# Second pass of the expert ups and the downs in one stage, with 256 instead of 192 tokens gathered row by row

## What is computed

```python
def one(xc):                                   # xc: normed tokens, 1024 wide
    ...                                        # 8 heads x top 16 of 128 x 128 experts: idx, g (softmax)
    act = gelu(einsum('nd,nhkd->nhk', xc, expert_u[idx]), approximate=False)
    return einsum('nhk,nhkd->nd', g * act, expert_v[idx])
```

## Time and profile before

| | us |
|---|---|
| median of 3 runs (2007.05 to 2012.56) | 2011.68 |
| the profiled execution: its own time | 2011.93 |
| its span in the profile | 2010.3 |
| mean granted TensorE clock | 0.977 |

### The profile page before, as it was taken

How to read it: one execution, slowest core, us unless ns; L and a number is a source line. 1 busy time by engine, 2 the same in 40 slices (tenths; PEclk the granted TensorE clock), 3 DMA queues, 4 the chain that set the end, 5 groups by cost and what they waited for, 6 DMA issues and landing times.

```text
span 2010.3 us, 39023 instructions
## 1 busy us (share of the span) xinstructions
PE 1904.8 (95%) x14702; PEld 1805.8 (90%) x14702; DVE 1390.1 (69%) x2528; ACT 856.2 (43%) x1119; POOL 1119.5 (56%) x755
## 2 busy tenths in 40 slices
PE   7988988888999999999999999999989999999998
PEld 6977764358999999999999999999989999999998
DVE  3669665432589888964446776465638999999996
ACT  4233664412213454556566555344433333333331
POOL 3323222223225888886768888778864555665630
PEclk8999999889999999999999999999998999999999
DMA  5434878761123777776867898998989999999993
GB/s 166 78 107 150 284 255 284 245 214 63 64 106 126 221 228 233 219 230 224 303 220 273 307 348 313 397 338 310 338 290 306 323 361 348 354 358 335 358 332 113
DMA packets 253534, 508.80 MB, mean 253 GB/s; under 512 B 51041, under 2 KB 172962, under 8 KB 232642
## 3 DMA queue, kind: packets, MB, share of 16 engines
q1 hardware_dynamic: 202930, 369.56, 54.3%
q0 software_dynamic: 44032, 134.35, 18.4%
q10 hardware_dynamic: 6416, 2.78, 1.0%
HBM read 442.77 MB, written 63.73 MB: 252 GB/s over the span
## 4 chain that ended last, share of the span: by engine, by line
PE 72%; DVE 10%; POOL 6%; DMA 4%; ACT 4%; issue 2%; DVEq 1%; SPq 1%; ACTq 0%; POOLq 0%
PE pair L1552 20%; PE pair L1553 20%; PE pair L1554 19%; PE pair L1883 4%; DVE conv L1082 3%; POOL w_lo L651 2%; PE pair L1697 2%; POOL v_rows L662 2%; DMA act<-acts 2%; DMA acts<-act_out 1%; POOL picked_a L655 1%; PE pair L1709 1%; DVE pair L1437 1%; DVE w_lo L1491 1%; PE pair L1749 1%
## 5 line engine op out<-in xcount | busy, mean ns | idle before, releaser
L1552 PE MATMUL pair<-x_hi,w_hi 128*128 128x256 f32 (+2 forms) x2560 | 752.5, 294 | 28.0 <-DVE x_lo L1038 16.2
L1553 PE MATMUL pair<-x_lo,w_hi 128*128 128x256 f32 (+2 forms) x2560 | 742.5, 290 | 0.0
L1554 PE MATMUL pair<-x_hi,w_lo 128*128 128x256 f32 (+2 forms) x2560 | 741.0, 289 | 0.0
L1552 PEld LDWEIGHTS pair<-x_hi,w_hi 128*128 128x128 f32 x2560 | 487.0, 190 | 33.5 <-issue 18.8
L1553 PEld LDWEIGHTS pair<-x_lo,w_hi 128*128 128x128 f32 x2560 | 486.4, 190 | 0.2
L1554 PEld LDWEIGHTS pair<-x_hi,w_lo 128*128 128x128 f32 x2560 | 484.7, 189 | 0.0
L1552 PE MATMUL pair<-a_hi,w_hi 128*128 128x352 f32 x1024 | 332.5, 325 | 12.9 <-DVE w_lo L1491 9.7
L662 POOL DMA_INDIRECT v_rows<-in_v_t,at_row x192 | 199.4, 1039 | 238.0 <-DVE pair L1437 205.2
L1553 PE MATMUL pair<-a_lo,w_hi 128*128 128x352 f32 x1024 | 331.5, 324 | 0.0
L1554 PE MATMUL pair<-a_hi,w_lo 128*128 128x352 f32 x1024 | 331.2, 323 | 0.0
L651 POOL TENSOR_TENSOR w_lo<-w_raw,w_hi 128x1024 fp32r<-128x1024 f32 x116 | 275.7, 2399 | 87.5 <-ACT w_hi L922 87.4
(11 more groups left out here) (219 smaller groups left out, 2735.6 us busy)
## 6 DMA issues: line engine op xcount, KB each, us to landing
w_raw<-in_u_t SPq DMA_DIRECT2D x85, 1024.0 KB, 5.6
v_raw<-in_u_t SPq DMA_DIRECT2D x43, 1024.0 KB, 5.3
w_raw<-in_v_t SPq DMA_DIRECT2D x128, 256.0 KB
v_raw<-in_v_t SPq DMA_DIRECT2D x128, 256.0 KB
gates<-g_out SPq DMA_DIRECT2D x11, 2048.0 KB, 10.7
act<-acts SPq DMA_DIRECT2D x64, 352.0 KB, 5.9
g_in<-gates SPq DMA_DIRECT2D x16, 1408.0 KB, 10.5
acts<-act_out SPq DMA_DIRECT2D x64, 288.0 KB, 7.1
```

Of the source, the lines that this page charges most:

```text
L1552: te.matmul(out, s_hi, m_hi, start=start, stop=False)
L1553: te.matmul(out, s_hi, m_lo, start=False, stop=False)
L1554: return te.matmul(out, s_lo, m_hi, start=False, stop=stop)
```

## The change

- NS becomes 256: tokens 0 to 255, which are those of pass one, are all gathered, in 2 x 128 slots; the dense part is 288 tokens, those of pass two. ALL_ROWS is 256. The move of half lists for 64 tokens (slots_moved) goes, and the list of token tile 1 is used as that of tile 0 is.
- Gates: 72 groups instead of 88, four in a step from step 46, so all within pass one.
- Pass two and the downs are one stage of 68 slots (ENDS). In a slot TensorE does half 0 of an up, block 0 of the down of the chunk four slots back (BESIDE), half 1, block 1. The gelus of the dense tokens stay in SBUF: no store and load of them.
- Split chunks of u and v take turns in three places (the third is x_hi/x_lo of the first 256 tokens, free by then); raw u and v have two buffers each. ups use PSUM banks 0 and 1, downs 2 and 3, one bank each.
- Low parts of u: on VectorE in the first four slots and then in two of three, else GpSimd. Low parts of v stay on VectorE. The 256 rows are spread evenly over the stage from its second step on.
- Outside: sigmoids at slot 15 instead of 20 and ahead of keep_output, finish_conv at 17 instead of 22, the copy of the next weights ahead of the square of a block instead of behind it.

```diff
-EXTRA = 64
-NS = P + EXTRA
+NS = FIRST
-GATES_FROM, GATES_PER_STEP = 47, 2
+GATES_FROM, GATES_PER_STEP = 46, 4
+BESIDE = 4
+ENDS = STEPS + BESIDE
+ROWS_FROM, ROWS_TO = 1, 63
 def on_vector(t):
-    return t % 4 == 0 if ROWS_FROM <= t < SPLIT_FROM else t >= SPLIT_FROM and t % 3 != 0
+    return t > STEPS and (t <= STEPS + BESIDE or t % 3 != 0)
+def rows_until(slot):
+    passed = (min(slot, BESIDE) + max(slot - STEPS, 0)) / 2 + max(min(slot, STEPS) - BESIDE, 0)
+    return int(min(max(ALL_ROWS * (passed - ROWS_FROM) / (ROWS_TO - ROWS_FROM), 0), ALL_ROWS))
+def gated_at(slot):
+    if slot < BESIDE:
+        return {2: (0, 1), 3: (2, 3)}.get(slot, ())
+    return (slot,) if slot < STEPS else ()
+def place_of_u(step):
+    return 2 * step % 3
+def place_of_v(c):
+    return (2 * (c + BESIDE) + 1) % 3
...
 # SP, after pass one
+            for parity in range(2):
+                sp.wait_ge(g_stored[parity], 16 * ((NG + 1 - parity) // 2))
+            load_gates(0, 0)
+            for parity in range(2):
+                sp.wait_ge(acts_stored[parity], 16 * STEPS // 2)
+            load_v(1)
+            load_gates(1, 1)
+            for slot in range(ENDS):
+                if slot + 3 < STEPS:
+                    wait_low_u(sp, STEPS + slot + 1)
+                    load_u(STEPS + slot + 3)
+                c = slot + 1 - BESIDE
+                if 0 <= c < STEPS - 2:
+                    sp.wait_ge(v_lo_done, c + 1)
+                    load_v(c + 2)
+                if slot % 4 == 3 and slot // 4 + 2 < STEPS // 4:
+                    sp.wait_ge(gated, 2 * slot + 2)
+                    load_gates(slot // 4 + 2, slot // 4 % 2)
 # GpSimd
+            for parity in range(2):
+                pool.wait_ge(acts_stored[parity], 16 * STEPS // 2)
+            for slot in range(ENDS):
+                for k in range(PIECE * slot, PIECE * slot + PIECE):
+                    if k < AHEAD:
                         fetch_unit(k)
+                mine = rows_added_at(slot)
+                for k in mine[:len(mine) // 2]:
                     fetch_ahead(k)
+                if slot + 1 < STEPS and not on_vector(STEPS + slot + 1):
+                    split_u(STEPS + slot + 1)
+                for k in mine[len(mine) // 2:]:
+                    fetch_ahead(k)
 # ScalarE
+            for slot in range(ENDS):
+                c = slot + 1 - BESIDE
+                if slot + 1 < STEPS:
+                    high_u(STEPS + slot + 1)
+                if slot < STEPS:
+                    gelu_out(STEPS + slot, 0)
+                    gelu_out(STEPS + slot, 1)
+                if 0 <= c < STEPS:
+                    high_v(c)
+                for step in gated_at(slot):
+                    high_a(step)
 # VectorE
+            for slot in range(ENDS):
+                c = slot - BESIDE
+                mine = rows_added_at(slot)
+                if c > 0:
+                    add_block(c - 1, 1)
+                if slot + 1 < STEPS and on_vector(STEPS + slot + 1):
+                    split_u(STEPS + slot + 1)
+                for k in mine[:len(mine) // 2]:
                     add_row(k)
+                if slot == TURN_FIRST + 2:
+                    add_total(0)
+                if c >= 0:
+                    add_block(c, 0)
+                for step in gated_at(slot):
+                    gate_acts(step)
+                if 0 <= c + 1 < STEPS:
                     split_v(c + 1)
+                for step in gated_at(slot):
+                    low_acts(step)
+                for k in mine[len(mine) // 2:]:
                     add_row(k)
 # TensorE
+            for slot in range(ENDS):
+                if slot == TURN_FIRST:
+                    turn_rows(0)
+                for half in range(2):
+                    if slot < STEPS:
+                        up(STEPS + slot, (half,))
+                    if slot >= BESIDE:
+                        down(slot - BESIDE, (half,))
```

More of the change, by code:

```diff
@@ L113, in splits_until, with u_buffer, u_loads, v_loads @@
     return mine if on_vector(t) else t + 1 - mine
-def stores_until(t):
-    return sum(32 if n < STEPS else 16 for n in range(t % 2, t + 1, 2))
+def u_buffer(t):
+    return t % 3 if t < STEPS else 1 - t % 2
+def u_loads(t):
+    return sum(1 for n in range(t + 1) if u_buffer(n) == u_buffer(t))
+def v_loads(c):
+    return c // 2 + 1
 def gate_groups(t):
@@ L355, in build_layer @@
     u_loaded = [sem(f"u_loaded{slot}") for slot in range(3)]
-    v_loaded = [sem(f"v_loaded{slot}") for slot in range(4)]
+    v_loaded = [sem(f"v_loaded{slot}") for slot in range(2)]
     g_loaded = [sem("g_loaded0"), sem("g_loaded1")]
@@ L373, in wait_low_u, with wait_place @@
         engine.wait_ge(u_lo_vector if on_vector(t) else u_lo_pool, 2 * splits_until(t) - 1 + j)
+    def wait_place(engine, step, c):
+        n = 2 * step if c is None else 2 * (c + BESIDE) + 1
+        engine.wait_ge(up_done, 2 * STEPS - 2 if n == 0 else 2 * STEPS)
+        for m in range(n - 3, -1, -3):
+            if m % 2 == 0 and m // 2 < STEPS:
+                engine.wait_ge(up_done, 2 * STEPS + m + 2)
+                return
+            if m % 2 and m // 2 >= BESIDE:
+                engine.wait_ge(down_done, 2 * (m // 2 - BESIDE) + 2)
+                return
     KEY_UNITS, VALUE_SLOTS = 12, 26
@@ L544, in _ @@
[L544 to L556, removed]
@@ L557, in _ @@
-            store_acts(PASSES - 1)
-            for parity in range(2):
[L559 to L570, removed]
-                    sp.wait_ge(v_lo_done, c + 1)
-                    load_v(2 * it + k // 4 + 1, k % 4)
-                if not last or k < 2:
-                    sp.wait_ge(a_done, 2 * c + 10)
-                    load_acts(c + 6, k % 2)
-                if not last and k % 4 == 3:
-                    sp.wait_ge(gated, 2 * c + 10)
-                    load_gates(2 * it + k // 4 + 3, (k // 4 + 1) % 2)
@@ L671, in fetch_ahead @@
                     fetch_row(k + RING)
-            for t in range(PASSES):
-                if not on_vector(t):
-                    split_u(t)
+            for t in range(STEPS + 1):
+                split_u(t)
                 if t == FETCH_FROM:
@@ L1895, in _ @@
             next_group = 3 * PH - 4
-            for t in range(PASSES):
+            for t in range(STEPS):
                 up(t)
@@ L1945, in _ @@
-            for quad in range(STEPS // 4 - 2, STEPS // 4):
-                for part in range(4):
-                    down(quad, quad % 2, part, quad == STEPS // 4 - 1 and part == 3)
+            te.wait_ge(rt_kept, NT - 2)
+            for slot in range(ENDS):
[6 more added lines that the diff above has]
+                        down(slot - BESIDE, (half,))
```

388 lines of the change are left out of this document (147 added, 241 removed).

## The result

The changed kernel takes 2014.93 us (median of 15 runs, 2008.65 to 2023.99); the kernel before took 2010.84 (15 runs). The ratio is 1.003 with a 95% interval of 1.0016 to 1.0044: slower by a fraction, +0.3% (+0.2%, 4 us, by the two medians) where +0.6% was forecast. The time lies inside the range. The profiled execution has a span of 2012.6 us.

What follows compares the result with a forecast made beforehand. GpSimd was taken to set the fused stage's pace: 1063 start + 7 + 886 GpSimd work + 5 + 36 loop idle + 6 + 1.3 + 17 = 2021, with 1.6 around 2023 us. Range 1960 to 2070; the forecast's own case 2005 to 2045.

Steps and rivals of the forecast that it cites:

- last fetch's end to its row added: End of the fused stage: the last gathered row lands in 6 us and is added in 1.3.
- Until the fused stage: Pass one: more gate groups (+33.8) and smaller terms sum to 35 us, so the fused stage starts at 1063 (1057 to 1070).
- the two terms of the edits outside: Before the fused stage: sigmoids moved to slot 15 give −2 us; moved high_w adds one ScalarE copy, 1.9.
- TensorE in the fused stage: 6144 matmuls of 288 columns take 819 us against 976 before; TensorE alone would win 157, less the 35.
- GpSimd sets the pace: Fused stage: GpSimd needs 14.3 us per full slot against TensorE's 12.8; its work sums to 886 (875 to 1000).
- Each stops a fetch ... I take 1.5: Fused stage: each of VectorE's 43 splits of u and 64 of v stops a GpSimd fetch, 1.5 us each, 160.
- 1.7 idle, 20 times: +36: Fused stage: after each GpSimd split, GpSimd waits 1.7 us for VectorE to use the row six places back; 0 to 40.
- VectorE's short operations of 0.5 us are left at nothing: Fused stage: VectorE's short operations are charged no stopped fetches; could cost 128 pairs × 0.3, up to +38 us.
- The signs: Right if GpSimd never pauses, one 2 to 3 us fetch per split, slots 14.5 to 15.5 us, TensorE idle 15%, start near 1063.
- A: Rival: GpSimd's bare sum, no loop idle because the six-row ring buffers it, 1.4 us per split; 1976, up to 2005; chance 0.22.
- B: Rival: TensorE stays the bound if a split costs GpSimd under 0.6 us; 1897, up to 1950; chance 0.12.
- C: Rival: the row ring turns into lockstep between GpSimd and VectorE, 64 × 0.8 = +51 us, up to 2070; chance 0.21.

Runs made afterwards that it cites:

- experiment 4: Kernel before with only the edits outside the fused stage (sigmoids at slot 15, finish_conv at 17, weight copies ahead of the squares): 2007.92 us, 0.9977.
- Experiment 5: Changed kernel without unit fetches (sums of gathered tokens lack the gelu) and with all low parts of u on VectorE: 1904.99 us, 0.9478.
- experiment 2: Changed kernel with all low parts of u in the fused stage made on VectorE, none on GpSimd: 1928.62 us, 0.9573.
- experiment 3: Changed kernel with GpSimd's split of u moved ahead of its slot's first row fetches, nothing removed: 1968.82 us, 0.979.
- 11: Changed kernel with GpSimd splitting u in every sixth slot instead of every third: 1970.75 us, 0.9782.
- experiment 6: Changed kernel with each VectorE split of u and v made as two instructions of 1024 columns instead of one of 2048: 2055.96 us, 1.0245.
- experiment 8: Changed kernel with a ring of five gathered rows instead of six: 2010.47 us, 1.0006.
- experiment 1: Changed kernel without the 256 unit fetches and the product of a gathered row's share with the gelu: 1946.99 us, 0.9673.
- experiment 9: Changed kernel with all low parts of u on VectorE and only the low parts of v as two instructions: 1922.03 us, 0.9531.

## Why the prediction was right or wrong

The pace setter came as forecast, and the sign, but the rise was half of the forecast one or less. What failed is the sum of GpSimd's time: the term for stopped fetches was 62 us too large, the term for idle time in the loop 54 us too small and with the wrong cause, and one effect was missing. The terms, against the profiled execution:

| step | forecast | measured |
|---|---|---|
| fused stage starts | 1063 | 1064.6 |
| first unit fetch | 1070 | 1067.8 |
| VectorE's splits stop fetches | 107 × 1.5 = 160 | 97.8 |
| idle of GpSimd at start | 5 | none beyond the 5.4 before the first fetch |
| idle in the loop | 36 | 103.1, or 90 less the 42 × 0.30 of issue that lie in it |
| last fetch's end to its row added | 7.3 | 1982.2 to 1995.6, 13.4 |
| last row to the end | 17 | 17.0 |

*Until the fused stage: the sum right, in part by luck.* 35 us were forecast and 36 came. But the two terms of the edits outside, −2 and +1.9, were −6 in the trace of experiment 4, so the rest, mainly the gate groups, came to about 42 and not 35. Single executions differ here by some us: the stage's first gelu starts at 1061 to 1068 in the traces of the versions. The wait for the first gate product in step 46, forecast at 3.5, is in the time line of TensorE:

```profile
894.25 2.07 PE L1862 MATMUL pair<-hot,hot 128*128 128x128 f32 x8 [3.51 <-DVE hot L1446]
```

*TensorE in the fused stage: right as a bound.* Experiment 5 reaches it.

*GpSimd sets the pace: right for this kernel.* Experiments 2, 3 and 11 take GpSimd's work away or only reorder it, and the time follows. Not by GpSimd alone, though: without its unit fetches VectorE, blocked by the splits, holds the time at 1947.

*"Each stops a fetch ... I take 1.5": the term of the sum that was mis-sized.* Measured 0.91, 62 us less. The stopping itself is shown, by the 80 fetches that end 0.81 to 0.84 us after a split and by the shorter ones of experiment 6. The price came from pass two, where GpSimd fetched without a pause; in the fused stage 27 of the 107 splits stop nothing. With fewer waits for rows more of them do: 100 of 107 in experiment 3, 117 of 127 in experiment 2. The 160 and the 36 were thus not independent: whoever lets an engine idle can't charge it the full stops as well.

*"1.7 idle, 20 times: +36": mis-sized the other way*, 90 to 103 us. The chain in the prediction let GpSimd run into VectorE at the end of the following slot, by 1.7 us. In the trace it is held one unit fetch behind its split, for 3.8 us in the piece shown and up to 4.9: without their issue these 20 waits are 71 us, the rest of the 90 lies at the start and the end of the stage. The cause named, the ring of six rows, is refuted by experiment 8. What is shown in its place is that GpSimd's split comes late, behind row fetches, so that TensorE waits for it (experiment 3: −46 us by order alone), and that it then blocks VectorE's gate product (experiment 1: 5.33 us for 0.45). How much of the 90 us is due to that blocking no run isolates, since experiment 2 takes the split and the blocking away together. VectorE was given 12.0 us per slot with its short products at their own 0.45; "VectorE's short operations of 0.5 us are left at nothing" looked only at what they do to GpSimd, not at what GpSimd does to them. The gate products cost 104.4 us instead of 53.2.

Together: −2 for the first fetch, −62 for the stops, +54 for the loop, −5 for the start and +6 for the last landing take the sum from 2021 to 2012, and the span is 2012.6. That 2023 came so close is luck: two errors of 62 and 54 us had opposite signs.

*The signs.* Of those named for a right forecast, the start of the stage and its slots (14.6 us) came. TensorE idles for 6 to 10% in the four stretches, not 15, and its 13 waits for GpSimd's split are 19 us of that. GpSimd is not busy or issuing all the time, and 29 fetches take 2 us or more beside the 107 splits, not one for each.

*The rivals.* A (1976) is not what happened, but experiment 3 (1968.8) shows it one reordering away. B needed a split to cost GpSimd under 0.6 us; it cost 0.91. That rule of the Trainium skill (SBUF — State Buffer, Who interferes with whom), by which a tensor_tensor leaves descriptor making alone, does not hold here: the 80 stopped fetches end with VectorE's instructions. The same section's sentence that a VectorE instruction with two SBUF inputs contends with a GpSimd one that reads SBUF agrees with the 5.33 us of experiment 1. Its other sentence, that issue order decides who blocks, is not borne out by that row: the product starts 0.23 us ahead of GpSimd's first half and is the one that waits, as do four others of that trace that start 0.54 to 0.55 us ahead; the recorded times of GpSimd are rough, though. C, slower by the ring, is refuted as a mechanism; the waits for VectorE's rows were more than the forecast's 36, but 103 us in all, where the kernel before had 205.

Of the gain on offer, 157 us of TensorE's time less 35, all was given back to GpSimd and VectorE in turn, and 4 us more. **The best versions** are experiment 9 (1922.0 us) and experiment 2 (1928.6 us), whose intervals overlap: 4.3 to 4.7% below the kernel before; both compute all that it computes.

## What to carry to other kernels

When stages are fused so that GpSimd fetches without a pause, take elementwise work with two SBUF operands off GpSimd first, even if the receiving engine looks fuller: here a split costs 4.7 us of GpSimd and 2.6 of VectorE besides (104.4 less 53.2 us of gate products, over 20 splits), against 2.3 us when VectorE makes it. Where an engine both fetches and feeds TensorE, put the piece that TensorE waits for ahead of the fetches (46 us here). And when a sum charges an engine for being stopped, check that it isn't also charged for idling at the same time.

## What was not expected of the hardware

- The blocking goes both ways and by whole instructions: a 0.45 us VectorE product took 2.79 us beside the second half of GpSimd's split and 5.33 us beside both halves, and no gap between the two let it through: all 20 products that met a split of the changed kernel ended behind its second half. There the longest took 4.83 us.
- A fetch is held until the end of VectorE's instruction: with two of 1.2 us in place of one of 2.29 the longest fetch fell from 2.98 to 1.98 us. The sum hardly gains by it as long as GpSimd doesn't wait: 155 to 138 us with v's splits halved.
- Cutting one instruction into two, 2.4 us together in place of 2.29, cost 41 to 112 us (u) or nothing (v). About half of the 112 us shows as pauses of TensorE inside products, with no releaser in the profile; the cause is open.
